# The split weight tiles moved by 16, 32, 48 and 64 bytes against the moving operands

## The chip, the cores and the metric

One core of a Trainium2 chip runs the whole program. The metric is the device time of one execution in microseconds (us), taken as the median of three runs.

## What is computed

The reference is a network of three mixers and one MLP on a sequence of 1024 tokens with 1024 channels, all in float32. Cut to what matters here:

```python
u = rms_norm(h, norm_g[0]); h = h + pooling_mixer(u, pool_w_in, pool_w, pool_scale, pool_w_out)
u = rms_norm(h, norm_g[1]); h = h + stick_breaking_mixer(u, sb_w_in, sb_w_out)   # 16 heads, causal
h = rms_norm(h, norm_f)
h = h + gated_deltanet(rmsnorm(h, norm_mix_g), gdn_w_in, conv_w, ..., gdn_w_out) # 8 heads, chunks
h = h + square(relu(rmsnorm(h, norm_mlp_g) @ mlp_w1)) @ mlp_w2
return rmsnorm(h, final_norm_g)
```

Nearly all the arithmetic is in the products with the weight matrices (`pool_w_in`, `sb_w_in`, `gdn_w_in`, `mlp_w1`, `mlp_w2` and the output projections).

## The kernel before

Activations lie transposed in SBUF: channels on the 128 partitions, tokens along the free axis. Each operand x of a large product is held as two parts, a rounded one (`hi`, type fp32r) and the rest x - hi (`lo`, fp32r). A product is then three matmuls into the same bank: rounded weights by rounded state, rounded weights by the rest of the state, the rest of the weights by the rounded state. The function `gemm` has them at lines 798 to 800. In each, the weights are the stationary operand, a 128x128 slice, and the state is the moving operand, 128x512. So every matmul has a weight load of its own, which the trace lists apart (PEld) and which runs while the matmul before it streams. The same three lines stand again at 816 to 818 (the first tile), 868 to 870 (pool output by halves), 897 to 899 (parts of projections that are put between the steps of attention and of the delta rule), 950, 1062, 1121, 1269 and 1320 to 1322 (the last MLP product, by blocks).

Weights come in tiles of 128x1024 float32 through two slots that alternate. SyncE's queue fills `weights_raw`. ScalarE rounds it into `weights_hi` (line 1349). VectorE writes the rest into `weights_lo` (line 1778). TensorE waits for `weights_lo` before the first matmul of a tile (line 785 and its like). The last product has three more, smaller tile pairs, `down_weights_hi` and `down_weights_lo`, beside halves of the four weight tiles (lines 123 and 124).

The program places its tiles by hand. `place` takes the next free byte of the partition and rounds a size up to 32. The start is byte 16576, which is 192 modulo 256. All large tiles have sizes that are multiples of 256, so `weights_raw`, `weights_hi`, `weights_lo` and `inv_rms` start at 192 modulo 256. Five small tiles follow, the gains of the norms, the identity, the mean matrix and the epsilons, and one step of 64 bytes (the line `at[0] += 64`) brings the states `state_a_hi` and `state_a_lo` to 192 modulo 256 again. What comes after them, `state_b`, `pooled`, `pool_y`, the queries, keys and values, is at 192 modulo 256 too. One family of moving operands is not: `weights_T_hi` and `weights_T_lo`, the attention weights turned (lines 936 to 938), come after four tiles of 513 elements and start at 64 modulo 256, while their stationary operands `v_hi` and `v_lo` start at 192. The slices of a stationary operand are 512 bytes apart and those of a moving one 2048, so each slice has the start of its tile modulo 256.

`identity` is the moving operand of the transposes (lines 810, 907, 924, 1080, 1282), and `mean_matrix` the stationary one of the sums of squares (845, 979, 1035). `inv_rms` scales what leaves the banks.

Of the kernel before, what the change touches and what calls it, by code (L numbers as in the profile page):

```python
# [5 lines left out]
F32, F32R = mybir.dt.float32, mybir.dt.float32r  # L6
ACT = mybir.ActivationFunctionType
P = 128
S, D, DI = 1024, 1024, 2048
HALF = 512  # L10
KC, TT = D // P, S // P
# [31 lines left out]
def build(nc, t, out):  # L43
    ctx = ExitStack()
    with ctx:
        at = [16576]
        def place(name, shape, dt=F32, offset=None):
            size = int(np.prod(shape[1:])) * 4
            if offset is None:
                offset = at[0]  # L50
                at[0] += (size + 31) // 32 * 32
            assert offset + size <= 229344, (name, offset + size)
            return nc.alloc_sbuf_tensor_at(name, shape, dt, offset=offset)
        def sem(name):
            return ctx.enter_context(nc.semaphore(name))
        raw = [place(f"weights_raw_{s}", [P, KC * P]) for s in range(2)]
        w_hi = [place(f"weights_hi_{s}", [P, KC * P], F32R) for s in range(2)]
        w_lo = [place(f"weights_lo_{s}", [P, KC * P], F32R) for s in range(2)]
        inv = place("inv_rms", [P, S])
        gains = place("norm_gains", [P, 5, KC])  # L60
        ident = place("identity", [P, P])
        mean_of = place("mean_matrix", [P, P])
        eps_col = place("eps_column", [P, 3])
        at[0] += 64
        A_hi = place("state_a_hi", [P, KC, S], F32R)
        A_lo = place("state_a_lo", [P, KC, S], F32R)
        free0 = at[0]
# [2440 lines left out]
```

## Time and profile before

| | |
|---|---|
| median of 3 runs | 3025.99 us (3024.34 to 3030.14) |
| the profiled execution | 3026.86 us, its span 3025.1 us |
| TensorE matmul busy | 2973.3 us, 98% |
| TensorE weight load busy | 2472.7 us, 82% |
| VectorE, ScalarE, GpSimd busy | 63%, 37%, 19% |
| mean granted TensorE clock | 0.994 |
| HBM read and written | 187.31 MB and 64.00 MB, 83 GB/s |

The duration of one matmul in the trace is the time until its result has left the array. Matmuls that follow each other overlap, so a duration (about 390 ns) is no measure of what a matmul costs. That is the distance from one start to the next, called the pitch below. The timeline gives the starts.

### The profile page before, as it was taken

Reading aid. Unit: us, or ns where it says so; the run is one execution under the profiler, and the core shown is the slowest. Engines: PE = TensorE matmul, PEld = TensorE weight load, DVE = VectorE, ACT = ScalarE, POOL = GpSimd, SP = SyncE. Lnnn points to the kernel's source line nnn. Section 1 sums busy time; section 2 is a strip of 40 time slices with the busy share of each in tenths; the row PEclk is TensorE's granted clock in tenths of the full one; section 3 lists DMA queues with packets and bytes.
Section 4 is the critical chain, followed back from the end, with each engine's and each line's share of the span. In section 5 each row is a group of like instructions: output and inputs, shape, how many; then the busy total and the mean of one; then the engine's idle time right before and its main releaser. Section 6 shows DMA issues by size and latency. Waiting matters only on the chain.

```text
span 3025.1 us, 41047 instructions
## 1 busy us (share of the span) xinstructions
PE 2973.3 (98%) x14498; PEld 2472.7 (82%) x14498; DVE 1911.9 (63%) x2278; ACT 1122.6 (37%) x1608; POOL 578.7 (19%) x1023
## 2 busy tenths in 40 slices
PE   8999999999999999998999999999999999999998
PEld 7888888878888888887887788888887888877886
DVE  6545454557676767777336666666655455577776
ACT  4212121245454454545234444444543111133333
POOL 1000000024344444444032322222212000000000
PEclk9999999999999999999999999999999999999999
DMA  4111112231111111112512211111121354576552
GB/s 112 50 44 54 42 55 42 49 98 43 35 49 49 35 49 35 49 35 80 184 43 51 94 39 38 38 38 38 38 80 56 121 185 149 191 267 213 195 194 84
DMA packets 330024, 252.51 MB, mean 83 GB/s; under 512 B 79560, under 2 KB 286408, under 8 KB 329680
## 3 DMA queue, kind: packets, MB, share of 16 engines
q1 hardware_dynamic: 328784, 251.28, 27.5%
q8 instruction: 54, 0.88, 0.1%
q14 instruction: 34, 0.28, 0.0%
q10 hardware_dynamic: 1152, 0.07, 0.0%
HBM read 187.31 MB, written 64.00 MB: 83 GB/s over the span
## 4 chain that ended last, share of the span: by engine, by line
PE 89%; DVE 4%; DMA 2%; issue 2%; POOL 1%; ACT 1%; SPq 0%; DVEq 0%; ACTq 0%; POOLq 0%
PE banks L798 12%; PE banks L799 12%; PE banks L800 12%; PE banks L897 9%; PE banks L899 9%; PE banks L898 9%; PE banks L1320 3%; PE banks L1322 3%; PE banks L1321 3%; PE banks L924 2%; PE banks L1156 1%; PE banks L917 1%; PE banks L936 1%; PE banks L938 1%; PE banks L1080 1%
## 5 line engine op out<-in xcount | busy, mean ns | idle before, releaser
L897 PE MATMUL banks<-state_a_hi,weights_hi 128*128 128x512 f32 x1296 | 545.5, 421 | 1.4 <-DVE projection_staged L1912 1.3
L899 PE MATMUL banks<-state_a_hi,weights_lo 128*128 128x512 f32 x1296 | 510.1, 394 | 0.0
L898 PE MATMUL banks<-state_a_lo,weights_hi 128*128 128x512 f32 x1296 | 507.2, 391 | 0.0
L1349 ACT ACTIVATE weights_hi<-weights_raw 128x1024 fp32r<-128x1024 f32 x194 | 204.6, 1055 | 565.5 <-PE banks L800 495.9
L1778 DVE TENSOR_TENSOR weights_lo<-weights_raw,weights_hi 128x1024 fp32r<-128x1024 f32 x194 | 261.4, 1348 | 111.1 <-ACT weights_hi L1349 108.4
L899 PEld LDWEIGHTS banks<-state_a_hi,weights_lo 128*128 128x128 f32 x1296 | 243.3, 188 | 55.0
L897 PEld LDWEIGHTS banks<-state_a_hi,weights_hi 128*128 128x128 f32 x1296 | 244.6, 189 | 40.9 <-issue 2.3
L898 PEld LDWEIGHTS banks<-state_a_lo,weights_hi 128*128 128x128 f32 x1296 | 245.4, 189 | 35.0 <-issue 0.5
L1897 DVE TENSOR_TENSOR_SCAN stick_left<-stick_left,eps_column 128x128 f32<-128x128 f32 (+1 forms) x192 | 243.5, 1269 | 40.3 <-POOL beta L661 34.0
L798 PE MATMUL banks<-state_a_hi,weights_hi 128*128 128x512 f32 x648 | 253.3, 391 | 3.0 <-DVE weights_lo L1778 3.0
L799 PE MATMUL banks<-state_a_lo,weights_hi 128*128 128x512 f32 x648 | 252.8, 390 | 0.0
L800 PE MATMUL banks<-state_a_hi,weights_lo 128*128 128x512 f32 x648 | 252.6, 390 | 0.0
L666 POOL TENSOR_TENSOR beta<-beta,stick_left 128x128 f32<-128x128 f32 (+1 forms) x192 | 167.9, 875 | 412.7 <-DVE stick_left L1897 403.0
L798 PE MATMUL banks<-state_b_hi,weights_hi 128*128 128x512 f32 x608 | 236.9, 390 | 0.0
L800 PE MATMUL banks<-state_b_hi,weights_lo 128*128 128x512 f32 x608 | 236.5, 389 | 0.0
L799 PE MATMUL banks<-state_b_lo,weights_hi 128*128 128x512 f32 x608 | 236.5, 389 | 0.0
L1423 ACT ACTIVATE weights_T_hi<-banks 128x128 fp32r<-128x128 f32 (+1 forms) x192 | 94.5, 493 | 230.9 <-PE banks L924 230.9
L1903 DVE TENSOR_TENSOR weights_T_lo<-banks,weights_T_hi 128x128 fp32r<-128x128 f32 (+1 forms) x192 | 103.8, 541 | 118.3 <-ACT weights_T_hi L1423 118.3
L1415 ACT ACTIVATE beta<-banks 128x128 f32<-128x128 f32 (+1 forms) x192 | 94.2, 490 | 162.7 <-PE banks L917 161.5
L798 PEld LDWEIGHTS banks<-state_a_hi,weights_hi 128*128 128x128 f32 x648 | 121.9, 188 | 30.1 <-issue 2.4
L800 PEld LDWEIGHTS banks<-state_a_hi,weights_lo 128*128 128x128 f32 x648 | 122.1, 188 | 25.5
L799 PEld LDWEIGHTS banks<-state_a_lo,weights_hi 128*128 128x128 f32 x648 | 122.1, 188 | 25.1
(412 smaller groups left out, 6055.7 us busy)
## 6 DMA issues: line engine op xcount, KB each, us to landing
weights_raw<-in_mlp_w_dram SPq DMA_DIRECT2D x48, 512.0 KB, 4.4
relu_blocks_dram<-relu_blocks_staged SPq DMA_DIRECT2D x16, 1536.0 KB, 6.1
weights_raw<-in_gdn_w_in_dram SPq DMA_DIRECT2D x33, 512.0 KB, 4.2
weights_raw<-in_pool_w_in_dram SPq DMA_DIRECT2D x32, 512.0 KB, 4.2
weights_raw<-in_sb_w_in_dram SPq DMA_DIRECT2D x32, 512.0 KB, 4.1
relu_blocks_dram<-relu_sums_staged SPq DMA_DIRECT2D x16, 1024.0 KB, 8.9
relu_b<-relu_blocks_dram SPq DMA_DIRECT2D x16, 1024.0 KB, 9.5
state_b_lo<-relu_blocks_dram SPq DMA_DIRECT2D x16, 1024.0 KB, 13.0
```

The lines of the kernel that those rows point to most:

```text
L666: ins = pool.tensor_tensor(b, b, left[c][:, HALF - w + 1:HALF + 1], ALU.mult)
L798: pe.matmul(psum[:, bank, :], whi, hi, start=(k == 0), stop=False)
L799: pe.matmul(psum[:, bank, :], whi, lo, start=False, stop=False)
L800: last = pe.matmul(psum[:, bank, :], wlo, hi, start=False, stop=(k == kc - 1))
L897: pe.matmul(psum[:, bank, :], whi, hi, start=(k == 0), stop=False)
L898: pe.matmul(psum[:, bank, :], whi, lo, start=False, stop=False)
L899: last = pe.matmul(psum[:, bank, :], wlo, hi, start=False, stop=(k == end - 1))
L1349: act.activation(w_hi[slot][:, :], raw[slot][:, :], ACT.Copy).then_inc(weights_hi, 1)
L1423: act.activation(aT_hi[r][:, 0:w // P, c * P:c * P + P], psum[:, 5 + n % 2, 0:w].rearrange("p (j q) -> p j q", q=P), ACT.Copy).then_inc(a_ ...
L1778: dve.tensor_tensor(w_lo[slot][:, :], raw[slot][:, :], w_hi[slot][:, :].bitcast(F32), ALU.subtract).then_inc(weights_lo, 1)
L1897: dve.tensor_tensor_scan(v, v, eps_col[:, 2:3].to_broadcast([P, w]), left[c][:, HALF:HALF + 1], ALU.mult, ALU.add).then_inc(stick_scanned, 1)
L1903: dve.tensor_tensor(aT_lo[r][:, 0:w // P, c * P:c * P + P], psum[:, 5 + n % 2, 0:w].rearrange("p (j q) -> p j q", q=P), hi, ALU.subtract). ...
```

## The change

The four tiles of the split weights are placed in the order hi 0, lo 0, hi 1, lo 1. Each `weights_hi` is allocated with four elements (16 bytes) more, and used from its fifth element on. With the rounding of sizes to 32 bytes the four start at 208, 224, 240 and 0 modulo 256, that is 16, 32, 48 and 64 bytes beyond the 192 at which the states start. The step of 64 bytes ahead of the states goes, since the tiles before it have grown by as much. So `state_a_hi` and all behind it stay at the byte where they were, and so do both `weights_raw`. `inv_rms`, the gains, the identity, the mean matrix and the epsilons move up by 64 bytes. No instruction, wait, size or order changes.

```diff
         raw = [place(f"weights_raw_{s}", [P, KC * P]) for s in range(2)]
-        w_hi = [place(f"weights_hi_{s}", [P, KC * P], F32R) for s in range(2)]
-        w_lo = [place(f"weights_lo_{s}", [P, KC * P], F32R) for s in range(2)]
+        w_hi, w_lo = [], []
+        for s in range(2):
+            w_hi.append(place(f"weights_hi_{s}", [P, 4 + KC * P], F32R)[:, 4:])
+            w_lo.append(place(f"weights_lo_{s}", [P, KC * P], F32R))
         inv = place("inv_rms", [P, S])
         gains = place("norm_gains", [P, 5, KC])
         ident = place("identity", [P, P])
         mean_of = place("mean_matrix", [P, P])
         eps_col = place("eps_column", [P, 3])
-        at[0] += 64
         A_hi = place("state_a_hi", [P, KC, S], F32R)
```

## Rows read from the trace of the kernel before

**Rows 1.** The page's first and second part: busy time of TensorE, its granted clock.
```profile
PE 2973.3 (98%) x14498; PEld 2472.7 (82%) x14498; DVE 1911.9 (63%) x2278; ACT 1122.6 (37%) x1608; POOL 578.7 (19%) x1023
...
PEclk9999999999999999999999999999999999999999
```

**Rows 2.** The page's chain that ended last, shares of the span by engine.
```profile
PE 89%; DVE 4%; DMA 2%; issue 2%; POOL 1%; ACT 1%; SPq 0%; DVEq 0%; ACTq 0%; POOLq 0%
```

**Rows 3.** TensorE's groups by form: line, names (moving, stationary), shape, count, busy, mean.
```profile
L897 PE MATMUL banks<-state_a_hi,weights_hi 128*128 128x512 f32 x1296 | 545.5, 421 | 1.4 <-DVE projection_staged L1912 1.3 <-DVE conv_in L2073 0.2
...
L798 PE MATMUL banks<-state_a_hi,weights_hi 128*128 128x512 f32 x648 | 253.3, 391 | 3.0 <-DVE weights_lo L1778 3.0
...
L798 PE MATMUL banks<-state_b_hi,weights_hi 128*128 128x512 f32 x608 | 236.9, 390 | 0.0
...
L924 PE MATMUL banks<-identity,beta 128*128 128x128 f32 x576 | 95.1, 274 | 5.0 <-POOL stick_left L676 2.0 <-POOL stick_left L671 1.8 <-POOL beta L666 1.2
L798 PE MATMUL banks<-pooled_hi,weights_hi 128*128 128x512 f32 x224 | 87.1, 389 | 0.0
...
L1320 PE MATMUL banks<-state_b_hi,weights_hi 128*128 128x512 f32 x128 | 50.3, 393 | 0.8 <-issue 0.8
...
L798 PE MATMUL banks<-pool_y_hi,weights_hi 128*128 128x512 f32 x96 | 37.3, 389 | 0.0
...
L1320 PE MATMUL banks<-relu_b,weights_hi 128*128 128x512 f32 x68 | 26.8, 394 | 0.0
...
L1320 PE MATMUL banks<-relu_t,weights_hi 128*128 128x512 f32 x60 | 24.8, 413 | 3.2 <-issue 3.2
```

**Rows 4.** Timeline from 500 us, a stretch of gemm: start, duration, engine, line.
```profile
500.23 0.39 PE L798 MATMUL banks<-state_a_hi,weights_hi 128*128 128x512 f32 x1
500.23 0.19 PEld L799 LDWEIGHTS banks<-state_a_lo,weights_hi 128*128 128x128 f32 x1
...
501.59 0.39 PE L798 MATMUL banks<-state_a_hi,weights_hi 128*128 128x512 f32 x1
```

**Rows 5.** Busy time by stretch: stretch, length, each engine busy (count), clock, DMA.
```profile
100.00:600.00 500.00, 500.00 (x2208) 414.15 (x2207) 266.91 (x287) 93.46 (x91) 0.96 (x1) 1.00 0.18 49
...
2400.00:2650.00 250.00, 250.00 (x1105) 207.01 (x1104) 133.42 (x159) 41.60 (x46) 0.00 (x0) 1.00 0.50 171
```

**Rows 6.** Timeline of TensorE amid attention: projections between shorter matmuls.
```profile
1302.14 0.40 PE L897 MATMUL banks<-state_a_hi,weights_hi 128*128 128x512 f32 x1
...
1303.53 0.38 PE L924 MATMUL banks<-identity,beta 128*128 128x128 f32 x2
...
1306.05 0.39 PE L898 MATMUL banks<-state_a_lo,weights_hi 128*128 128x512 f32 x1
...
1306.96 0.39 PE L899 MATMUL banks<-state_a_hi,weights_lo 128*128 128x512 f32 x1
```

**Rows 7.** Timeline of TensorE, attention weights by values; 11 pitches from first to last.
```profile
1309.15 0.39 PE L937 MATMUL banks<-weights_T_lo,v_hi 128*128 128x512 f32 x1
...
1310.30 0.40 PE L936 MATMUL banks<-weights_T_hi,v_hi 128*128 128x512 f32 x1
1310.54 0.40 PE L937 MATMUL banks<-weights_T_lo,v_hi 128*128 128x512 f32 x1
...
1311.70 0.40 PE L897 MATMUL banks<-state_a_hi,weights_hi 128*128 128x512 f32 x1
```

**Rows 8.** Timeline of TensorE, full float32 passes of the sums of squares.
```profile
1619.41 1.88 PE L1035 MATMUL banks<-squares_o,mean_matrix 128*128 128x512 f32 x4
1621.13 1.45 PE L1035 MATMUL banks<-mixed_staged,mean_matrix 128*128 128x512 f32 x3
```

**Rows 9.** Groups by form of ScalarE and VectorE that write the moved tiles.
```profile
L1349 ACT ACTIVATE weights_hi<-weights_raw 128x1024 fp32r<-128x1024 f32 x194 | 204.6, 1055 | 565.5 <-PE banks L800 495.9 <-PE banks L1064 26.3 <-PE banks L870 23.8
...
L1778 DVE TENSOR_TENSOR weights_lo<-weights_raw,weights_hi 128x1024 fp32r<-128x1024 f32 x194 | 261.4, 1348 | 111.1 <-ACT weights_hi L1349 108.4
```

**Rows 10.** Who TensorE waited for: total us, times, longest.
```profile
PE banks L798 <- DVE weights_lo L1778: 3.0, 2, 1.7
```

## The prediction

> **What bounds the kernel now.** I read the page first. TensorE's matmuls are busy for 98% of the span, and its granted clock is full in every slice [rows 1], so neither idle time nor the lower clock level is there to be won or lost. The chain that ended last runs through TensorE for 89% of the span [rows 2]. So whatever each matmul takes more or less is paid in full, and whatever the other engines do is paid only where TensorE waits for it.
>
> Then I read what TensorE does. The groups by form give the counts [rows 3]. I sort them in two kinds. Steady work is that of lines 798 to 800 and 1320 to 1322: triples of 128x512 matmuls with nothing between them, 648 + 608 + 224 + 96 of the first and 128 + 68 + 60 of the second that use the moved tiles. That is 1832 triples, 5496 matmuls. (The down tiles of line 1320 don't move, and some hundred triples of other lines are left out.) Interrupted work is that of lines 897 to 899: 1296 triples, 3888 matmuls, put between short matmuls and transposes of attention and of the delta rule.
>
> Then I read the pitch, from start to start. In the steady stretch six matmuls take from 500.23 to 501.59, 226.7 ns each, and the load of the next weights starts with the matmul [rows 4]. The stretch from 100 to 600 us holds 2208 matmuls in 500 us, 226.4 ns each, and a stretch with four times its DMA traffic 1105 in 250 us, 226.2 ns [rows 5]. So the pitch doesn't care whether DMA, VectorE or ScalarE are at work. It is TensorE's own.
>
> A matmul of 512 columns at the full 2.4 GHz would take 213.3 ns. The steady pitch is 13.4 ns longer. Some of that is a cost that every matmul has. The full float32 passes, which take a column in 1/1.2 ns, give it: four of them lie from 1619.41 to 1621.13, 430 ns each against 426.7, so 3.3 ns [rows 8]. What is left, about 10.1 ns in each fp32r matmul, is there only when the moving operand streams at full speed above a weight load. I read it as the two streams meeting in SBUF. That makes it something that an address could change.
>
> Amid attention the pitch is another. Six matmuls from 1302.14 to 1303.53 take 231.7 ns each. After some matmuls without a short one between them the pitch falls to the steady one: four from 1306.05 to 1306.96 take 227.5 [rows 6]. The same tiles at the same addresses thus have a good pitch, into which a long run settles, and a worse one while it hasn't.
>
> **The change, part by part.** No instruction or wait is added, removed or moved, so the whole effect is durations.
>
> The stationary operands of the 5496 and the 3888 matmuls start 16, 32, 48 or 64 bytes further than now, against moving operands that stay at 192 modulo 256. Now the distance is 0 modulo 256. The trace has one family with another distance, the attention weights times values, where the moving operand is at 64 and the stationary one at 192, a distance of 128. Its eleven pitches from 1309.15 to 1311.70 are 231.8 ns in the mean, one of them 240 (1310.30 to 1310.54), and they don't settle [rows 7]. That is 5.1 ns above 226.7. From both sides, then: the pitch can fall to 216.6, by 10.1 ns, if the streams no longer meet, and rise to 240, by 13.3 ns, if each matmul is like the worst one. I take +5.1, since the family at another distance is the nearest row that there is, and since it agrees with the unsettled pitch of the present tiles: a distance of zero looks like what lets a run settle. The three matmuls of a triple also have unequal distances after the change (16, 16, 32 or 48, 48, 64), which speaks against a common rhythm.
>
> Steady work: 5496 x 5.1 ns = 28.0 us. Interrupted work is mostly at 231.7 already, as bad as the other family, and loses only where it now settles. I take one matmul in three for settled, judged from the two stretches of [rows 6]: 3888 / 3 x 5.1 = 6.6 us (none to all would be 0 to 19.8).
>
> The Trainium skill says otherwise ("SBUF — State Buffer", "Who interferes with whom"): TensorE has two independent read ports, one for the moving operand and one for the weights, and never waits on anyone. Its page "TensorE: Matmul & The Clock Gate" ("Wait — 56ns, not 53.3ns?") gives 215.7 ns from start to start for 512 columns at full clock. The trace shows 11 ns more, so here the ports seem not to be free of each other. By the page the sum would be zero.
>
> Rounding and rest: ScalarE's 194 roundings take 1055 ns each, VectorE's 194 subtractions 1348 [rows 9]. They now write or read tiles that start, some of them, at an odd multiple of 16 bytes. I cost this at nothing. ScalarE sits idle for 565.5 us before these roundings, nearly all of it for TensorE to free the tile. TensorE waits for the subtraction for 3.0 us in all, twice [rows 10]. If each of both took a tenth longer, 0.24 us would lie on the way of a tile; with both slots ahead it stays hidden but for those two, so half a microsecond. A gain is worth as little.
>
> The 64 bytes of `inv_rms`, the gains and the identity: the identity moves against the 576 transposes of attention [rows 3] and others. The identity is at a distance from the turned tiles before and after, so I take nothing; 5 ns on each of the 576 either way would be 2.9 us. Weight tiles land where they landed, so no DMA changes.
>
> The sum is 28.0 + 6.6 = 34.6 us, on the profiled execution's 3026.86 us (span 3025.1, median 3025.99, so it stands 0.9 us above the median and I leave it): 3061.5 us.
>
> **The rivals.**
> *The address of the weights plays no part.* The 10.1 ns would then be a cost of fp32r itself, and the unsettled pitches an effect of the short matmuls alone. For it speaks that the pitch of [rows 5] is the same with pooled, state_a and state_b as moving operands, and that the family of [rows 7] also runs amid short matmuls, so it may be unsettled for that reason and not for its distance. Against it, that its eleven pitches in a row don't settle where those of [rows 6] do. It gives 3026.9 us. It is also what the skill's page on the ports asks for; the trace bears that out only in so far as other engines leave the pitch alone.
>
> *The streams meet less often: faster.* With the weights some tens of bytes ahead, a load could run without touching what the matmul above it reads. In full it gives 5496 x 10.1 = 55.5 us, and in interrupted work 3888 x (231.7 - 216.6) = 58.7 us, down to 2912.7. I hold half of the steady part for likelier, 27.8 us, since two of the four tiles may sit well and two badly: 2999 us. It decides as soon as the mean steady pitch is under 226.7; a fall of 1.1 ns would be 6 us. Against it: the weights run over 512 bytes, two rounds of 256, so a shift moves the meetings more than it removes them.
>
> *The change doesn't do what it says* would be tiles that landed elsewhere, with the pitch as before: it falls together with the first rival.
>
> **How the numbers follow.** My forecast, slower by lost settling, gets 0.49; no effect 0.23; fewer meetings 0.28. Predicted is 3061.5. The range goes up to half way between 5.1 and 13.3 ns on the steady work, 9.2 x 5496 = 50.6, + 6.6 = 57.2, so 3084. Down it reaches past the rival of no effect to four fifths of the 55.5 us, 44.4, so 2982; about 0.14 of the 0.28 lies above that. The forecast's own range is 3035 to 3084, since less than 8 us would ask for a pitch within 1.5 ns of the present one. About 0.2% (6 us) is what a measurement of this kernel can tell from no change: faster 0.28, same 0.23, slower 0.49.
>
> **What would show it.** In the timeline of a gemm stretch the pitch would be about 232 ns instead of 226.7, and the count in 100 to 600 us about 2157 instead of 2208. It should differ between the two slots, 16/16/32 against 48/48/64: if slots alternate between 227 and a worse pitch, only some distances hurt. The pitch amid attention should hardly move, and ScalarE's and VectorE's means should stay at 1055 and 1348 ns. A steady pitch of exactly 226.7 proves the first rival; one below it, and fewer than 231.7 amid attention, the second. If TensorE begins to wait for the split, I was wrong on the cover.

## The result and the profile after

The changed kernel takes 3062.84 us (median of 4 runs, 3059.91 to 3063.5) against 3027.14 us for the kernel before (4 runs). The ratio is 1.0115 with a 95% interval of 1.01 to 1.0129: slower by 35.7 us. Its profiled execution has a span of 3061.6 us, 36.5 us longer than before. The forecast was 3061.5 us for the time. One execution of the kernel before (8218.68 us) and one of the kernel with everything lower by 32 bytes (3294.0 us), both in the last round of experiments, lie far off all others and are left out of the ratios.

The page, first part and chain, which answer to [rows 1, 2]:

```profile
PE 3009.9 (98%) x14498; PEld 2481.2 (81%) x14498; DVE 1911.5 (62%) x2278; ACT 1123.1 (37%) x1608; POOL 577.4 (19%) x1023
...
PEclk9999999999999999999999999999999999999999
...
PE 90%; DVE 4%; issue 2%; ACT 1%; POOL 1%; DMA 1%; SPq 0%; DVEq 0%; ACTq 0%; POOLq 0%
```

The instructions are the same in number on every engine, and the mean granted clock is 0.994 as before. TensorE alone is busy 36.6 us longer, which is the whole loss. Lines stand one further down than in the kernel before, so line 799 is the old 798.

Busy time by stretch in the kernel after, the same stretches as [rows 5]:

```profile
100.00:600.00 500.00, 500.00 (x2155) 406.92 (x2154) 260.37 (x279) 87.69 (x85) 0.00 (x0) 1.00 0.17 48
2400.00:2650.00 250.00, 250.00 (x1078) 203.39 (x1077) 132.79 (x158) 40.83 (x44) 0.00 (x0) 1.00 0.48 166
```

In 500 us there are 2155 matmuls instead of 2208, so the mean pitch (start to start) went from 226.4 to 232.0 ns. The timeline of the kernel after, in the stretch of [rows 4], shows it matmul by matmul:

```profile
499.76 0.40 PE L799 MATMUL banks<-state_a_hi,weights_hi 128*128 128x512 f32 x1
499.99 0.39 PE L800 MATMUL banks<-state_a_lo,weights_hi 128*128 128x512 f32 x1
500.23 0.40 PE L801 MATMUL banks<-state_a_hi,weights_lo 128*128 128x512 f32 x1
...
502.32 0.39 PE L801 MATMUL banks<-state_a_hi,weights_lo 128*128 128x512 f32 x1
```

Nine pitches from 500.23 to 502.32 make 232.2 ns each.

This is a mean over two slots that differ. A tile of weights is 48 matmuls of gemm, and the slots alternate. Three starts of tiles in the same trace, of slot 0 (distances of 16, 16, 32), of slot 1 (48, 48, 64) and of slot 0 again:

```profile
156.96 0.40 PE L799 MATMUL banks<-pool_y_hi,weights_hi 128*128 128x512 f32 x1
...
168.15 0.40 PE L799 MATMUL banks<-pool_y_hi,weights_hi 128*128 128x512 f32 x1
...
179.25 0.40 PE L799 MATMUL banks<-state_a_hi,weights_hi 128*128 128x512 f32 x1
```

The 48 pitches of slot 0 are 233.1 ns in the mean, those of slot 1 231.3, and the tiles of gemm alternate between these two values in all its stages. The trace keeps the starts to 1 ns. In slot 0 the pitches repeat every six matmuls, 233, 233, 234, 231, 233 and 236 ns, from the start of the tile to all but its last. In the kernel before every tile has 227, 227, 226 over and over, which is one pitch of 226.7 as far as 1 ns can tell. So the stream isn't restless after the change. It settles at once, in another cycle with a longer mean.

The groups by form of TensorE, after, to be held against [rows 3]. In a dense stream the recorded duration grows with the pitch, so the means can be compared:

```profile
L898 PE MATMUL banks<-state_a_hi,weights_hi 128*128 128x512 f32 x1296 | 547.8, 423 | 1.3 <-DVE projection_staged L1913 1.2 <-DVE conv_in L2074 0.2
...
L799 PE MATMUL banks<-state_a_hi,weights_hi 128*128 128x512 f32 x648 | 257.5, 397 | 1.5 <-DVE weights_lo L1779 0.9 <-DVE stream_again L2149 0.6
...
L799 PE MATMUL banks<-state_b_hi,weights_hi 128*128 128x512 f32 x608 | 241.3, 397 | 0.0
```

Gemm's group over state_a went from 391 to 397 ns, that over state_b from 390 to 397. The interrupted group of line 898 went only from 421 to 423.

The kernel carries its own control, the last product (lines 1321 to 1323), which alternates between the moved tiles and the down tiles, which stayed. Groups of TensorE from 2780 to 2980 us, after:

```profile
L1323 PE MATMUL banks<-state_b_hi,weights_lo 128*128 128x512 f32 x89 | 35.2, 396 | 0.0
L1321 PE MATMUL banks<-state_b_hi,weights_hi 128*128 128x512 f32 x89 | 35.2, 395 | 0.0
L1322 PE MATMUL banks<-state_b_lo,weights_hi 128*128 128x512 f32 x89 | 35.1, 394 | 0.0
L1323 PE MATMUL banks<-state_b_hi,down_weights_lo 128*128 128x512 f32 x78 | 30.3, 389 | 0.0
L1321 PE MATMUL banks<-state_b_hi,down_weights_hi 128*128 128x512 f32 x77 | 30.0, 389 | 0.0
```

The same groups before, from 2750 to 2950 us:

```profile
L1320 PE MATMUL banks<-state_b_hi,weights_hi 128*128 128x512 f32 x93 | 36.2, 389 | 0.0
...
L1320 PE MATMUL banks<-state_b_hi,down_weights_hi 128*128 128x512 f32 x78 | 30.3, 389 | 0.0
```

With the same moving tile `state_b`, matmuls on moved weights take 394 to 396 ns, and those on weights that stayed 389, as all of them did before. So the loss follows the moved tile, within one stretch of one execution.

The engines that write the moved tiles didn't change, as [rows 9] had them at 1055 and 1348 ns:

```profile
L1350 ACT ACTIVATE weights_hi<-weights_raw 128x1024 fp32r<-128x1024 f32 x194 | 204.9, 1056 | 588.5 <-PE banks L801 516.9
L1779 DVE TENSOR_TENSOR weights_lo<-weights_raw,weights_hi 128x1024 fp32r<-128x1024 f32 x194 | 262.1, 1351 | 112.6 <-ACT weights_hi L1350 110.1
```

### The profile page after: what moved, and what is told of

Read it like the earlier page. It is cut to its first block, busy times and chain, and to the rows that moved or that the text cites. A ratio compares the mean times of both kernels' runs of the same rounds, so it can differ in the third digit from the quotient of the medians.

```text
span 3061.6 us, 41047 instructions
## 1 busy us (share of the span) xinstructions
PE 3009.9 (98%) x14498; PEld 2481.2 (81%) x14498; DVE 1911.5 (62%) x2278; ACT 1123.1 (37%) x1608; POOL 577.4 (19%) x1023
## 4 chain that ended last, share of the span: by engine, by line
PE 90%; DVE 4%; issue 2%; ACT 1%; POOL 1%; DMA 1%; SPq 0%; DVEq 0%; ACTq 0%; POOLq 0%
PE banks L799 12%; PE banks L801 12%; PE banks L800 12%; PE banks L898 9%; PE banks L899 9%; PE banks L900 9%; PE banks L1321 3%; PE banks L1323 3%; PE banks L1322 3%; PE banks L925 2%; PE banks L1157 1%; PE banks L937 1%; PE banks L939 1%; PE banks L938 1%; PE banks L918 1%
## 5 line engine op out<-in xcount | busy, mean ns | idle before, releaser
L1350 ACT ACTIVATE weights_hi<-weights_raw 128x1024 fp32r<-128x1024 f32 x194 | 204.9, 1056 | 588.5 <-PE banks L801 516.9
L1779 DVE TENSOR_TENSOR weights_lo<-weights_raw,weights_hi 128x1024 fp32r<-128x1024 f32 x194 | 262.1, 1351 | 112.6 <-ACT weights_hi L1350 110.1
L799 PE MATMUL banks<-state_a_hi,weights_hi 128*128 128x512 f32 x648 | 257.5, 397 | 1.5 <-DVE weights_lo L1779 0.9
L801 PE MATMUL banks<-state_a_hi,weights_lo 128*128 128x512 f32 x648 | 255.2, 394 | 0.0
L800 PE MATMUL banks<-state_a_lo,weights_hi 128*128 128x512 f32 x648 | 255.2, 394 | 0.0
L799 PE MATMUL banks<-state_b_hi,weights_hi 128*128 128x512 f32 x608 | 241.3, 397 | 0.0
L801 PE MATMUL banks<-state_b_hi,weights_lo 128*128 128x512 f32 x608 | 239.3, 394 | 0.0
L800 PE MATMUL banks<-state_b_lo,weights_hi 128*128 128x512 f32 x608 | 239.0, 393 | 0.0
L801 PEld LDWEIGHTS banks<-state_a_hi,weights_lo 128*128 128x128 f32 x648 | 124.1, 191 | 29.2
```

The costliest lines, as they stand in the source:

```text
L799: pe.matmul(psum[:, bank, :], whi, hi, start=(k == 0), stop=False)
L800: pe.matmul(psum[:, bank, :], whi, lo, start=False, stop=False)
L801: last = pe.matmul(psum[:, bank, :], wlo, hi, start=False, stop=(k == kc - 1))
L1350: act.activation(w_hi[slot][:, :], raw[slot][:, :], ACT.Copy).then_inc(weights_hi, 1)
L1779: dve.tensor_tensor(w_lo[slot][:, :], raw[slot][:, :], w_hi[slot][:, :].bitcast(F32), ALU.subtract).then_inc(weights_lo, 1)
```

## The experiments

All take the kernel before as their base. "Distance" is the start of the stationary tile less that of the moving tile, modulo 256 bytes. The theory D on trial, my forecast's, is that only a distance of zero lets a run of matmuls settle at 226.7 ns. "The helper" is `split_tile` of the second experiment. In the three runs with two distances (64 and 128, 160 and 224, 8 and 32) the tiles lie in the order of the change, hi 0, lo 0, hi 1, lo 1. In all others they keep the order of the kernel before, hi 0, hi 1, lo 0, lo 1.

### Small tiles alone

```diff
+        at[0] += 64
         inv = place("inv_rms", [P, S])
         ...
-        at[0] += 64
```

> Only inv_rms, the gains, the identity, the mean matrix and the epsilons move up by 64 bytes, as in the change; the split weight tiles stay at 192 modulo 256. My theory, that the distance between the stationary and the moving operand is the cause: 3027 us, steady pitch 226.7 ns, count of matmuls from 100 to 600 us 2208. The rival, that the small tiles cost something: between 3027 and 3063 us, with the steady pitch of gemm unchanged and the loss at the transposes or the banks' evictions.

Measured: 3025.87 us (10 runs), ratio 0.9998 (0.9988 to 1.0008). The stretch from 100 to 600 us holds 2207 matmuls. The 64 bytes of `inv_rms`, the gains, the identity and the mean matrix cost nothing, so the loss comes from where the split tiles lie.

### All four split tiles by 16

```diff
+        w0 = 16576 + 2 * KC * P * 4
+        def split_tile(name, place_no, shift):
+            pad = shift % 32 // 4
+            x = nc.alloc_sbuf_tensor_at(name, [P, pad + KC * P], F32R, offset=w0 + place_no * KC * P * 4 + shift - 4 * pad)
+            return x[:, pad:]
-        w_hi = [place(f"weights_hi_{s}", [P, KC * P], F32R) for s in range(2)]
-        w_lo = [place(f"weights_lo_{s}", [P, KC * P], F32R) for s in range(2)]
+        w_hi = [split_tile(f"weights_hi_{s}", n, d) for s, n, d in ((0, 0, 16), (1, 1, 16))]
+        w_lo = [split_tile(f"weights_lo_{s}", n, d) for s, n, d in ((0, 2, 16), (1, 3, 16))]
+        at[0] = w0 + 4 * KC * P * 4 + 64
         ...
-        at[0] += 64
```

The small tiles lie 64 bytes up, as in the change.

> All four split tiles 16 bytes beyond 192 modulo 256, so the three matmuls of a triple have equal distances; the small tiles are where the change has them. If it is the distance alone that must be zero: as the change, 3063 us, steady pitch about 232 ns. If it was the unequal distances within a triple (16, 16, 32) that keep the run from settling: 3027 us, with one steady pitch of 226.7 ns, or another single value.

Measured: 3052.99 us, ratio 1.01 (1.007 to 1.013), and a thing that neither expectation had. The four executions took 3046.46, 3059.53, 3065.03 and 3045.95 us. Busy time by stretch and, below it, two places of the timeline of the same execution:

```profile
100.00:600.00 500.00, 500.00 (x2208) 414.01 (x2207) 266.84 (x287) 93.05 (x91) 0.96 (x1) 1.00 0.18 49
2400.00:2650.00 250.00, 250.00 (x1073) 202.42 (x1072) 132.06 (x157) 42.05 (x46) 0.00 (x0) 1.00 0.47 162
```

```profile
500.02 0.39 PE L803 MATMUL banks<-state_a_hi,weights_hi 128*128 128x512 f32 x1
...
501.38 0.39 PE L803 MATMUL banks<-state_a_hi,weights_hi 128*128 128x512 f32 x1
...
2499.91 0.39 PE L803 MATMUL banks<-state_b_hi,weights_hi 128*128 128x512 f32 x1
...
2501.31 0.39 PE L803 MATMUL banks<-state_b_hi,weights_hi 128*128 128x512 f32 x1
```

One stretch runs at 1.36 / 6 = 226.7 ns throughout, the other, with the same tiles, code and distance, at 1.40 / 6 = 233.3 ns throughout. At this distance a run can settle at either pitch and then keeps it for hundreds of microseconds. In this trace every tile of gemm up to 640 us has 226.7 ns and every one from 1463 us on 233.3, so the pitch changed once, across the attention stage. Equal distances within a triple are not enough for the good one, so the rival (unequal distances as the only cause) falls. But D as I put it, "never at another distance", falls too.

### Only the rest tiles by 16

The same helper with a shift of 0 for both `weights_hi` and of 16 for both `weights_lo`.

> The rounded tiles stay at 192 modulo 256, only the rest tiles lie 16 bytes further. One load in three has a distance of 16. Distance theory, if any wrong load unsettles the run: nearly the whole loss, 3055 to 3063 us, all three pitches of the triple at 229 to 234 ns. If each load costs by itself: a third of the loss, 3039 us, with only the matmul that streams above the load of the rest longer than 226.7 ns.

Measured: 3050.82 us, ratio 1.009 (1.0063 to 1.0118), single executions 3040.55, 3058.17, 3043.46 and 3059.66 us. Two stretches of its profiled execution:

```profile
2499.76 0.39 PE L803 MATMUL banks<-state_b_hi,weights_hi 128*128 128x512 f32 x1
2499.99 0.40 PE L804 MATMUL banks<-state_b_lo,weights_hi 128*128 128x512 f32 x1
2500.23 0.39 PE L805 MATMUL banks<-state_b_hi,weights_lo 128*128 128x512 f32 x1
2500.46 0.40 PE L803 MATMUL banks<-state_b_hi,weights_hi 128*128 128x512 f32 x1
...
2501.16 0.39 PE L803 MATMUL banks<-state_b_hi,weights_hi 128*128 128x512 f32 x1
```

There six matmuls take 1.40 us, 233 ns each, 232.2 over whole tiles. The lengthening isn't confined to the one that streams above the displaced load: by the starts to 1 ns the pitches repeat every twelve, between 228 and 236 ns, with no one of the three spared. At 500 us the same kernel runs at 226.7, the stretch from 100 to 600 us holding 2207 matmuls. So one wrong load in three can put the whole triple into the longer cycle, not a third of it. Here the pitch changed across the delta rule, between the tiles from 1606 and from 2314 us. The executions, 19 us apart, say that it isn't the same in each, but of each kernel one was traced.

### Weights and state_a by -16

The helper with -16 for all four; `weights_raw` 32 bytes lower to make room; and

```diff
-        A_hi = place("state_a_hi", [P, KC, S], F32R)
-        A_lo = place("state_a_lo", [P, KC, S], F32R)
+        A_at = at[0]
+        A_hi, A_lo = (nc.alloc_sbuf_tensor_at(f"state_a_{n}", [P, 4 + KC * S], F32R, offset=A_at + c * KC * S * 4 - 32)[:, 4:].rearrange("p (k s) -> p k s", s=S)
+                      for c, n in enumerate(("hi", "lo")))
+        at[0] = A_at + 2 * KC * S * 4
         ...
```

> The four split tiles and the two tiles of state_a lie 16 bytes lower, at 176 modulo 256; state_b, pooled and pool_y stay at 192. So products over state_a have a distance of zero at another place modulo 256, the others a distance of -16 with the same weights. Distance theory: steady pitch 226.7 ns over state_a (100 to 600 us where the weights meet state_a), about 232 over state_b (2400 to 2650 us: some 1078 matmuls instead of 1105), in all about 3027 + (608 + 224 + 96 + 256) x 3 x 5.1 ns = 3045 us. If what counts is that a tile starts at a multiple of 32 or 64: both about 232 ns, 3063 us or more.

Measured: 3039.95 us, ratio 1.004 (1.0026 to 1.0054). The time lies near the expected 3045, and the profile shows that this was luck, since the parts are the wrong way round. Timeline at two places:

```profile
224.67 0.39 PE L806 MATMUL banks<-state_a_hi,weights_hi 128*128 128x512 f32 x1
...
226.52 0.39 PE L808 MATMUL banks<-state_a_hi,weights_lo 128*128 128x512 f32 x1
...
300.05 0.39 PE L808 MATMUL banks<-pool_y_hi,weights_lo 128*128 128x512 f32 x1
...
301.41 0.39 PE L808 MATMUL banks<-pooled_hi,weights_lo 128*128 128x512 f32 x1
```

Over `state_a`, at a distance of zero but both at 176 modulo 256, eight pitches make 231.3 ns each. Over `pool_y` and `pooled`, at a distance of -16, six make 226.7. So a distance of zero isn't sufficient: the place matters as well, at 176, the one place tried that is no multiple of 32. Whole tiles over state_a have 230.0 to 233.3 ns, never 226.7.

### Distances of 64 and 128

The helper with -192 (which is +64 modulo 256) for the first slot and -128 for the second, the start of all at 16384, the tiles behind the weights unmoved.

> The tiles of the first slot lie 64 bytes beyond 192 modulo 256 (192 bytes lower), those of the second 128 (128 bytes lower); small tiles and states where they were, weights_raw 192 bytes lower. All starts are multiples of 64. Theory M, after the first runs (the start of each operand against multiples of 64 decides how many pitches a run may settle into, and at multiples of 64 there is only the good one): 3027 us, 226.7 ns in both slots. Distance theory D (only a distance of zero modulo 256 settles for certain): 3045 to 3065 us, with steady pitches of 231 to 233 ns in one slot or both.

Measured: 3067.15 us, ratio 1.0135 (1.0118 to 1.0152), four executions within 3066.62 to 3068.51. From 100 to 600 us there are 2149 matmuls, 232.7 ns each, and the tiles of the first slot have 233.3 ns, those of the second 232.4. The time is 2 us beyond D's range. Theory M, that multiples of 64 bytes are all good, falls.

### Distances of 160 and 224

The helper with -96 and -32; `weights_raw` 96 bytes lower.

> The tiles of the first slot 96 bytes lower (distance 160), those of the second 32 bytes lower (distance 224): odd multiples of 32, all else as before but weights_raw 96 bytes lower. Theory M: unsettled or settled by chance, 3030 to 3065 us, since the weights don't start at a multiple of 64; in the profile stretches of 226.7 ns and stretches of 231 to 233. Theory D: all of gemm at 231 to 233 ns, 3055 to 3065 us. If 32 bytes are as good as 64: 3027 us.

Measured: 3075.2 us, ratio 1.0158 (1.0141 to 1.0175), executions from 3073.11 to 3077.13, 2145 matmuls from 100 to 600 us (233.1 ns), both slots within 0.2 ns of that. It is the slowest of all, beyond both expectations. In the first slot the pitches repeat every three, 232, 238 and 230 ns: a cycle as regular as the good one, with a mean of 233.3.

### Distances of 8 and 32

The helper with 8 and 32, the small tiles 64 bytes up.

> The tiles of the first slot 8 bytes beyond 192 modulo 256, those of the second 32; the small tiles 64 bytes up as in the change. Both theories: not the good pitch throughout, 3035 to 3065 us. If 8 bytes are too few to matter (half of the smallest step of the change), the first slot stays at 226.7 ns and only the second is longer, some 3040 us.

Measured: 3063.27 us, ratio 1.0121 (1.0105 to 1.0138), executions from 3062.63 to 3063.95, 2157 matmuls (231.8 ns). That mean alone doesn't say which slot pays. The starts of three tiles do, first slot, second slot, first slot:

```profile
157.63 0.39 PE L803 MATMUL banks<-pool_y_hi,weights_hi 128*128 128x512 f32 x1
...
168.70 0.40 PE L803 MATMUL banks<-pool_y_hi,weights_hi 128*128 128x512 f32 x1
...
179.90 0.39 PE L803 MATMUL banks<-state_a_hi,weights_hi 128*128 128x512 f32 x1
```

The 48 pitches at a distance of 8 are 230.6 ns in the mean, those at 32 bytes 233.3. So eight bytes are enough, beside a slot at 32.

### The turned attention weights at 192

```diff
+        at[0] += 128
         aT_hi, aT_lo = (...
```

> The turned attention weights (lines 936 to 938) start 128 bytes later, at 192 modulo 256 as their stationary operands; nothing else moves. My prediction leaned on this family as the nearest row. If its distance of 128 was what kept it from settling: its pitches fall from 231.8 to 226.7 ns after some five matmuls, for 96 triples 1.0 us at most, so the time stays 3027 us; the trace decides. If it was only the short matmuls around it: its pitches stay at 229 to 236 ns.

Measured: 3027.13 us (10 runs), ratio 1.0 (0.9991 to 1.001). The timeline of the family, to be held against [rows 7]:

```profile
1310.01 0.40 PE L938 MATMUL banks<-weights_T_lo,v_hi 128*128 128x512 f32 x1
...
1311.86 0.39 PE L937 MATMUL banks<-weights_T_hi,v_hi 128*128 128x512 f32 x1
...
1312.54 0.39 PE L898 MATMUL banks<-state_a_hi,weights_hi 128*128 128x512 f32 x1
1312.76 0.39 PE L899 MATMUL banks<-state_a_lo,weights_hi 128*128 128x512 f32 x1
```

The first eight pitches make 231.3 ns each. Only then, with three pitches in 0.68 us (226.7 each), has the run settled, when the family ends. At a distance of 128 its eleven pitches had been 231.8. So distance zero does let it settle, but eleven matmuls between short ones are too few to profit. The means are alike, the single pitches are not. To 1 ns those of [rows 7] are 233, 231, 229, 230, 232, 241, 233, 230, 232, 228 and 230. With a distance of zero they are 233, 236, 224, 231, 236, 228, 233, 230, and then 227, 227, 226. And the second slot of the run with 64 and 128, a long stream at the family's own distance of 128, repeats 230, 232, 241, 233, 231, 231, 229. So [rows 7] did show the cycle of its distance, and not just a short run that hadn't settled yet.

### Everything by -32, everything by -64

```diff
-        at = [16576]
+        at = [16576 - 32]
```

> Every tile of the program lies 32 bytes lower: weights and moving operands all at 160 modulo 256, each distance as before. If only the distance counts: 3027 us and 226.7 ns. The run with both operands at 176 modulo 256 spoke against that; if the place itself counts as well, and an operand must start at a multiple of 64: 3055 to 3065 us, steady pitches of 230 to 234 ns.

> Every tile lies 64 bytes lower, at 128 modulo 256, each distance as before. If the place counts only within 64 bytes, or not at all: 3027 us, 226.7 ns. If 192 modulo 256 itself is what the operands need: 3055 to 3065 us.

Measured: 3027.44 us, ratio 0.9998 (0.9988 to 1.0008), and 3026.97 us, ratio 1.0001 (0.9991 to 1.0011). Both hold 2208 matmuls from 100 to 600 us. With the first the weights are at 160 modulo 256, where the second slot's were in the run with distances of 160 and 224; there, with the states at 192, they were slow. So among the multiples of 32 tried (128, 160, 192) it is the distance that counts, not the place.

### All four by -16

The helper with -16 for all four, states at 192; `weights_raw` 32 bytes lower.

> All four split tiles 16 bytes lower than before (distance -16, or 240), the states at 192, the small tiles where they were. In the run with state_a lowered too, products at this distance had 226.7 ns. If a distance of -16 is as good as zero: 3027 us with little spread. If it settles by chance, as +16 did: executions between 3027 and 3065 us, stretches of 226.7 and of about 233 ns in the profile. If it doesn't settle: 3063 us.

Measured: 3032.38 us (10 runs), ratio 1.0015 (1.0005 to 1.0024), single executions from 3026.88 to 3038.2. The profiled one has:

```profile
499.80 0.39 PE L804 MATMUL banks<-state_a_hi,weights_hi 128*128 128x512 f32 x1
...
501.17 0.39 PE L804 MATMUL banks<-state_a_hi,weights_hi 128*128 128x512 f32 x1
```

1.37 / 6 = 228.3 ns, and 2191 matmuls from 100 to 600 us (228.2 ns). That is a third pitch, between the two, and every tile of gemm has it. The run with state_a lowered too had 226.7 at this distance in two stages and 228.3 in a third. The other executions here, down to 3026.88 us, may have had more at 226.7; no trace of them was taken. Of all distances other than zero it is the mildest.

### Half the weight load

```diff
-                            pe.matmul(psum[:, bank, :], whi, hi, start=(k == 0), stop=False)
-                            pe.matmul(psum[:, bank, :], whi, lo, start=False, stop=False)
-                            last = pe.matmul(psum[:, bank, :], wlo, hi, start=False, stop=(k == kc - 1))
+                            pe.matmul(psum[0:64, bank, :], whi[:, 0:64], hi, start=(k == 0), stop=False)
+                            pe.matmul(psum[0:64, bank, :], whi[:, 0:64], lo, start=False, stop=False)
+                            last = pe.matmul(psum[0:64, bank, :], wlo[:, 0:64], hi, start=False, stop=(k == kc - 1))
```

> The three matmuls of gemm (lines 798 to 800) take only the first 64 of the 128 columns of each weight slice, so half of each product's output channels are left out, and the load of the next weights is half as long; the addresses are as before. My theory says that the 13.4 ns above 213.3 come from the load meeting the moving operand: with half the load a steady pitch of about 216.6 + 10.1 / 2 = 221.7 ns, or the next value that a run can settle into. If the 13.4 ns are a cost of fp32r matmuls themselves: 226.7 ns as before, and the same time.

Measured: 3042.76 us in one execution. Timeline and stretch:

```profile
500.01 0.40 PE L799 MATMUL banks<-state_a_lo,weights_hi 128*64 128x512 f32 x1
500.01 0.13 PEld L800 LDWEIGHTS banks<-state_a_hi,weights_lo 128*64 128x64 f32 x1
500.25 0.39 PE L800 MATMUL banks<-state_a_hi,weights_lo 128*64 128x512 f32 x1
...
501.39 0.40 PE L799 MATMUL banks<-state_a_lo,weights_hi 128*64 128x512 f32 x1
```

```profile
100.00:600.00 500.00, 500.00 (x2178) 300.41 (x2176) 263.48 (x283) 90.23 (x88) 0.00 (x0) 1.00 0.17 48
```

Half of each product's outputs are left out. The load record shrinks from 190 to 130 ns, and the pitch is 1.38 / 6 = 230 ns, longer than 226.7. Neither 221.7 nor 226.7 ns came. So the excess over 213.3 ns isn't the same for every fp32r matmul of 512 columns, and it isn't proportional to the load either. The edit also halves the partitions of the bank that are written, so that the load alone did it isn't shown. It is one execution.

## Why the prediction was right, and where it wasn't

**The bound.** Right. TensorE's busy time grew by 36.6 us and the span by 36.5. No other engine's work changed. (The second stretch of [rows 5] has 3.5 times the DMA rate of the first, not four times; the reading stands.)

**The steady work.** I had 5.1 ns on 5496 matmuls. For gemm over the two states the groups' busy times grew from 253.3 + 252.8 + 252.6 + 236.9 + 236.5 + 236.5 = 1468.6 to 257.5 + 255.2 + 255.2 + 241.3 + 239.3 + 239.0 = 1487.5 us on 3768 matmuls, so 5.0 ns each. Over all of lines 798 to 800 the distances from start to start summed to 1077.8 us before and 1101.2 after in the two traces, 23.4 us against 4728 x 5.1 = 24.1. Line 1320's moved part seems to fall short, with 768 x 5.1 = 3.9 us expected and 1.0 measured by the same sum (180.1 to 181.1). But without the few pitches over 300 ns its mean went from 227.3 to 232.2 ns, which is 3.8 us on 768. The rest was hidden by the clock. In the trace before, twelve of these matmuls ran at the lower level of 1.2 GHz, 427 ns from start to start, after TensorE had been idle for 3.2 us:

```profile
2725.00:2731.00 6.00, 5.25 (x12) 4.18 (x13) 3.17 (x6) 0.63 (x1) 0.00 (x0) 0.50 1.12 294
```

After the same idle time the trace of the changed kernel has the full clock there (1.00 from 2758 to 2764 us). The term was right, and the sum of one pair of traces hid it.

**The interrupted work.** 6.6 us forecast with a third of the matmuls taken for settled; the sum over lines 897 to 899 grew by 4.8 us (947.0 to 951.7). That is right in kind and 1.8 us too much.

**The sum.** The two terms of my sum, 34.6 us, measured 23.4 + 1.0 + 4.8 = 29.2. What I had put at nothing made up for it. The other lines with moved weights are 216 triples and not some hundred, and grew by 3.3 us (157.6 to 160.9). Another 4 us are in lines whose own tiles didn't move, 2.5 of them in line 917 (in seven pitches that hold a wait) and 1.5 in lines 936 to 938. So the mechanism gave most of the number, and that it came within 2 us is in part luck.

**The nearest row.** The 231.8 ns of [rows 7] against 232.0 to 232.2 measured. The row did show what another distance does, as the run with the turned weights at 192 and the slot at 128 tell. It was in the cycle of its own distance, though, and not unsettled as I had it. That the cycles of the change's distances, 233.1 and 231.3 ns, have nearly the same mean as that at 128 was luck. Over whole tiles the other slow cycles seen lie between 228.3 and 233.4 ns.

**Distance zero lets a run settle.** This was my mechanism, and it is half right. A distance of zero does give the short pitch: a common shift of weights and states by 32 or 64 bytes cost nothing, and distances of 8 and 32, of 64 and 128, and of 160 and 224 were slow in each of their four executions, by 1.2 to 1.6%. But the slow streams aren't unsettled. They repeat as strictly as the good one, tile after tile, in another cycle. At 16 and -16 a stretch has the good cycle in some stretches and not in others, and at 176 modulo 256 a distance of zero didn't give it. "Only a distance of zero settles" was too strong, and "lost settling" the wrong picture. What the change lost is the short cycle. The 256 itself holds so far: the weights start 256 bytes off the states modulo 512, the down tiles 0 off `state_b`, and both have about 227 ns before.

**Unequal distances within a triple.** Not needed for a loss: the uniform 16 loses 1%, and slots with one distance each, of 32 and of 64 bytes, had 233.3 ns in the runs above. What takes the good cycle away for good was not separated. The four kernels at another distance whose executions agree within 5 us and whose traces never show 226.7 in gemm (the change, 64 and 128, 160 and 224, 8 and 32) all have a distance that differs between the two slots, and all have the tile order hi, lo, hi, lo. Those with the same distances in both slots (16, only the rest by 16, -16) can hold a good cycle, or one close to it, and vary from execution to execution by 11 to 19 us. No kernel has the one without the other, say 64 bytes in both slots, or the new order at a distance of zero. So that the distance costs is shown, and that it alone costs all of the 1.2% is not. The sign I had named, that the two slots would differ, did appear, with 233.1 and 231.3 ns. Neither is at the good pitch, so it isn't that only some of the distances hurt.

**The cover.** Right: ScalarE 1056 and VectorE 1351 ns, and TensorE's wait for the subtraction fell to 0.9 us.

**The rivals.** "No part" is excluded by the interval. "Fewer meetings" is excluded as well, and no distance tried gave a steady stretch with a mean pitch under 226.7 ns. Behind it stood my reading of the 10.1 ns as two streams that meet in SBUF. That is not shown. That the stationary tile's place matters is: with the states unmoved the pitch follows it. But half the load, with half the outputs, didn't shorten the pitch. What takes the 10.1 ns at the best pitch stays open, and so does what picks one of two cycles at 16 bytes. Since no kernel tried beats the one before, there was none to recommend.

## What to carry to other kernels

In a dense stream of fp32r matmuls, measure the pitch from start to start, not durations, tile by tile, and look for the cycle in which it repeats: a mean over two buffers can hide two cycles. Put stationary and moving tiles at the same start modulo 256 bytes; here that was good at 128, 160 and 192 and not at 176, and every other distance was slower in the median, by 0.15 to 1.6% of the whole kernel. A placement that times well once may have the good cycle by chance, so take several executions, and a trace of more than one stretch, before it is kept.

## What the runs showed that was not expected

A back-to-back stream of these matmuls runs in a cycle of at most twelve pitches that repeats to within 1 ns, and its mean goes with the distance: 226.7 ns at zero with both tiles at 128, 160 or 192, 230.6 at 8 bytes, 233.3 at 32 and 64, 232.4 at 128. The same instructions on the same addresses can have more than one such cycle. With all split tiles 16 bytes off, one execution had 226.7 ns for 500 us and 233.3 ns for 250 us, and the executions differ by 19 us in all. At -16 there was a third, 228.3 ns. In these traces the cycle changed only where other work broke the stream or another moving tile took over, never from tile to tile over the same one, apart from the two slots' own. The kernel before holds one, 226.7, in each of its long stretches. And a shift of only 8 bytes in one slot, with 32 in the other, costs 1.2%.
